# Mixture-of-experts layer: a wide expert's rows are brought out behind the next expert's gate and up product

## The chip, the cores and the metric

The kernel runs on one core of a Trainium2 chip. The metric is the time of one execution in device microseconds, taken as the median of several runs; lower is better. Five engines run programs of their own and meet through semaphores: TensorE (PE in the rows; its weight loads are PEld), VectorE (DVE), ScalarE (ACT), GpSimd (POOL) and SyncE (SP), which only issues transfers here.

## The reference

One decoder layer in float32 over 1024 tokens of width 1024. Two mixers and an output projection come first; behind them stands the part that this document is about, a feed-forward layer of 32 experts of which each token takes four:

```python
logits = xf @ router_w + router_b
top_val, top_idx = lax.top_k(logits, 4)
gates = softmax(top_val)
...
gu = xb @ w_gu[e] + b_gu[e]                  # 1024 -> 2048
gate, up = split(gu, 2)
gate = minimum(gate, 7.0); up = clip(up, -7.0, 7.0)
y = ((up + 1.0) * (gate * sigmoid(1.702 * gate))) @ w_down[e] + b_down[e]
...
out = zeros(...).at[buf_tok].add(y * buf_gate[:, None])    # sum of each token's four experts
```

The layer ends with a residual sum and a last norm.

## The kernel before

The experts are ordered by how many tokens they got, and each place in that order has a fixed number of rows (224, 204, 196, ... 98, 88). They are worked off in the order largest, smallest, second largest, second smallest, and so on (`ORDER`), so step r of the loop over 32 steps is a **wide** expert (two tiles of up to 128 rows, 132 to 224 rows together) at even r up to 28, and a **narrow** one (one tile, 88 to 128 rows) at every odd r and at r = 30. There are 15 wide ones, and each is followed by a narrow one.

TensorE's part of one step is: `gate_up` in eight blocks m = 0 to 7, each into one of four PSUM banks (`bank(m % 4)`; `gu_bank` says that a bank is free again); then `rows_in`, the transposes (line 1743) of the next expert's gathered rows; then the down product. A narrow expert's (`down_rows`, line 1778) comes out with rows on the partitions and is finished there. A wide expert's (`down`, line 1793) comes out transposed; ScalarE moves it to `yv`, and TensorE has to turn it back in `rows_out` (line 1752): for each of two tiles j, two halves of four 128x128 transposes, each half into one bank (`bank(6)` and `bank(7)`). VectorE scales a half by the gate while it moves it to `yt` (line 1919), and this gives the bank back (`tr_bank`). Both tiles use the same two banks, so the transposes of tile 1 wait for the moves of tile 0.

The rows of wide expert r are turned in step r + 1, the narrow one: TensorE does tile 0 behind block m = 3 of that step's gate and up product and tile 1 behind m = 4. VectorE's `clamps` goes through the same eight blocks one behind TensorE: two moves out of PSUM (lines 1935 and 1936; the second gives the bank back), a third operation (1939), and from m = 2 on it first waits until GpSimd has finished block m - 2 (`hT`). Its `rows_out` calls also stand behind its m = 3 and m = 4. GpSimd's `gated` makes two products for each block (1603 and 1606). Behind m = 5, `scatter_main` waits for `yt` and adds the previous expert's rows into memory (line 1594, one indirect transfer for each tile). At the head of each step GpSimd waits until the rows of the expert two steps back have landed (`y_out`), reads the list of the next expert's rows (1574) and gathers them (1581); all of that stands ahead of this step's `gated`.

The weights (12.6 MB for each expert) come in through SyncE's queue as the slots come free.

Of the kernel before, what the change touches and what calls it, by code (L numbers as in the profile page):

```python
# [30 lines left out]
ROWS = tuple(WIDTHS[r] for r in ORDER)  # L31
TILES = tuple(-(-w // P) for w in ROWS)
# [23 lines left out]
def program(nc, x, norm_mix_g, w_in, gm_norm_g, gm_ws, gm_bs, dn_conv_w, dn_a_log, dn_dt_bias,  # L56
# [6 lines left out]
    with ctx:  # L63
# [5 lines left out]
        def S(name, slot=None):  # L69
            key = name if slot is None else f"{name}_{slot}"  # L70
            if key not in sems:
                sems[key] = nc.alloc_semaphore(name=key)
            return sems[key]
# [44 lines left out]
        def cut(cols, at=None):  # L118
            a = used[0] if at is None else at
            if at is None:  # L120
                used[0] += cols
            assert a + cols <= AW, (a, cols)
            return arena[:, a:a + cols]

        def r3(ap, n):
            return ap.rearrange("p (a b) -> p a b", a=n)
# [64 lines left out]
        rec = [cut(4).rearrange("p (j c) -> p j c", j=2) for _ in range(3)]  # L191
# [4 lines left out]
        yv = r3(cut(2048), KT)  # L196
# [10 lines left out]
        def bank(n):  # L207
            return ps[:, n, :]
# [1278 lines left out]
        LAST = NE - 1  # L1487
# [10 lines left out]
        def tiles_to(r):  # L1498
            return sum(TILES[:r])

        def wide_to(r):
            return sum(n == 2 for n in TILES[:r])
# [65 lines left out]
        def _(pool):  # L1568
# [19 lines left out]
            def scatter(rows, b, n):  # L1588

                pool.wait_ge(S("yt"), b + 1)  # L1590
                pool.sem_inc(S("scattering"), 1)
                for j in range(-(-n // P)):
                    p = min(P, n - j * P)
                    pool.indirect_dma_start(h_dram, bass.IndirectOffsetOnAxis(ap=rows[0:p, j, 0:1], axis=0),  # L1594
                                            yt[0:p, j, :], None, compute_op=ALU.add).then_inc(S("y_out"), 16)
# [11 lines left out]
                    between(m)  # L1607

            def scatter_main(r, m):
                if r >= 0 and m == 5 and r + 1 < LAST:  # L1610
                    if r:
                        pool.wait_ge(S("y_out"), 16 * tiles_to(r))
                    scatter(idx[r % 3], r, ROWS[r])
# [113 lines left out]
        def _(pe):  # L1727
# [7 lines left out]
            def rows_in(b, before, wide, tiles):  # L1735

                for j in range(tiles):
                    pe.wait_ge(S("xin", j), 16 * (wide if j else b) + 16)
                    for r in range(2):
                        if j == 1:  # L1740
                            pe.wait_ge(S("gu_bank", r), 2 * b + 1)
                        for k in range(4):
                            last = t_.transpose(bank(4 * (1 - j) + r)[:, k * P:(k + 1) * P],  # L1743
                                                xin[:, j, (4 * r + k) * P:(4 * r + k + 1) * P], ident)
                        last.then_inc(S("xT_ps", r), 1)

            def rows_out(j, b, before):

                for r in range(2):
                    pe.wait_ge(S("tr_bank", r), before + (j + 1))  # L1750
                    for k in range(4):
                        last = t_.transpose(bank(6 + r)[:, k * P:(k + 1) * P], yv[:, 4 * r + k, j * P:(j + 1) * P], ident)  # L1752
                    last.then_inc(S("yt_ps", r), 1)

            def gate_up(b, n, between):

                for m in range(8):
                    g, c = m // 2, (m % 2) * P
                    pe.wait_ge(S("gu_bank", m % 4), 2 * b + m // 4 + 1)
                    for q in range(2):  # L1760
                        if m % 2 == 0:
                            pe.wait_ge(S(f"w_in{q}", g), 16 * b + 16)
                        for k in range(KT):
                            for c0, c1 in (((0, P),) if n > P else ((0, P // 2), (P // 2, P))):
                                last = t_.matmul(bank(m % 4)[c0:c1, q * CAP:q * CAP + n],  # L1765
                                                 wslot[g][:, k, 256 * q + c + c0:256 * q + c + c1],
                                                 xT[:, k, 0:n], start=(k == 0), stop=(k == KT - 1))
                    last.then_inc(S("gu_ps", m % 4), 1)
                    between(m)

            def down_rows(r):
                for q in range(2):
                    pe.wait_ge(S("w_in0", 4 + q), 16 * r + 16)
                    pe.wait_ge(S("tr_bank", q), tiles_to(r) + 1)
                    for k in range(KT):
                        if q == 0:
                            pe.wait_ge(S("hT"), 8 * r + k + 1)
                        last = t_.matmul(bank(6 + q), hT[:, k, 0:P], wslot[4 + q][:, k, :], start=(k == 0), stop=(k == KT - 1))  # L1778
                    last.then_inc(S("yt_ps", q), 1)

            def down(b, n, before, wide):
                for d in range(8):
                    g, c = 4 + d // 4, (d % 4) * P
                    if d % 4 == 0:
                        pe.wait_ge(S("w_in0", g), 16 * b + 16)
                    if d < 2:
                        pe.wait_ge(S("tr_bank", d), before + 1)
                    else:
                        pe.wait_ge(S("yv"), 8 * wide + d - 1)
                    for k in range(KT):  # L1790
                        if d == 0:
                            pe.wait_ge(S("hT"), 8 * b + k + 1)
                        last = t_.matmul(bank(6 + d % 2)[:, 0:n], wslot[g][:, k, c:c + P], hT[:, k, 0:n],  # L1793
                                         start=(k == 0), stop=(k == KT - 1))
                    last.then_inc(S("down", d % 2), 1)

            def rows_out_main(r, m):
                if r < 0 or TILES[r] == 1:
                    return
                if m == 3:  # L1800
                    pe.wait_ge(S("yv"), 8 * wide_to(r) + 8)
                    rows_out(0, r, tiles_to(r))
                if m == 4:
                    rows_out(1, r, tiles_to(r))

            rows_in(0, 0, 0, TILES[0])
            for r in range(NE):
                pe.wait_ge(S("xT_sb"), 2 * tiles_to(r + 1))
                gate_up(r, ROWS[r], lambda m: rows_out_main(r - 1, m))
                if r + 1 < NE:  # L1810
                    rows_in(r + 1, tiles_to(r + 1), wide_to(r + 1), TILES[r + 1])
                if TILES[r] == 2:
                    down(r, ROWS[r], tiles_to(r), wide_to(r))
                else:
                    down_rows(r)
# [12 lines left out]
        def _(dve):  # L1828
# [86 lines left out]
            def rows_out(j, before, of):  # L1915

                for r in range(2):
                    dve.wait_ge(S("yt_ps", r), before + (j + 1))
                    v.tensor_scalar(yt[:, j, 512 * r:512 * (r + 1)], bank(6 + r), of[:, j, 1:2], None, ALU.mult).then_inc(S("tr_bank", r), 1)  # L1919
# [25 lines left out]
            def rows_out_narrow(r):  # L1945
                dve.wait_ge(S("y_out"), 16 * tiles_to(r))
                b = narrow_to(r)
                dve.wait_ge(S("bd_in", b % 2), 16 * (b // 2 + 1))
                for q in range(2):
                    half = yt[:, 0, 512 * q:512 * (q + 1)]  # L1950
                    dve.wait_ge(S("yt_ps", q), tiles_to(r + 1))
                    v.tensor_tensor(half, bank(6 + q), bd_row[b % 2][:, 512 * q:512 * (q + 1)], ALU.add).then_inc(S("tr_bank", q), 1)
                dve.drain()
                dve.sem_inc(S("bd_used"), 1)
                v.tensor_scalar(yt[:, 0, :], yt[:, 0, :], rec[r % 3][:, 0, 1:2], None, ALU.mult).then_inc(S("yt"), 1)

            def rows_out_main(r, m):
                if r < 0:
                    return
                if TILES[r] == 1:  # L1960
                    if m == 3 and r + 1 < LAST:
                        rows_out_narrow(r)
                    return
                if m == 3:
                    if r:
                        dve.wait_ge(S("y_out"), 16 * tiles_to(r))
                    rows_out(0, tiles_to(r), rec[r % 3])
                if m == 4:
                    rows_out(1, tiles_to(r), rec[r % 3])
                    dve.drain()  # L1970
                    dve.sem_inc(S("yt"), 1)

# [134 lines left out]
```

## Time and profile before

| | |
|---|---|
| Time, median of 3 runs | 2297.16 us (2294.94 to 2298.45) |
| The profiled execution's own time | 2294.84 us |
| Its span in the profile | 2293.2 us |
| TensorE busy in the span | 97% (2216.3 us) |
| Weight loads of TensorE | 80% |
| VectorE / GpSimd / ScalarE busy | 33% / 26% / 16% |
| Granted TensorE clock, mean | 0.985 of 2.4 GHz |
| The experts' part of the span | 712 to 2293 us |

An engine's busy share tells how much of the span it had an instruction in work. The chain of waits follows the work back from the last instruction. Where TensorE is idle in the experts' part, something else sets the time there.

### The profile page before, as it was taken

The page shows a single profiled execution, that of the slowest core. Times are in us where ns is not written, and L with a number is a line of the kernel's source. Part 1 is how long each engine was busy: PE and PEld are TensorE (multiplying, and loading weights), DVE is VectorE, ACT ScalarE, POOL GpSimd, SP SyncE. Part 2 cuts the span into 40 slices and gives each one's busy share as a digit, 9 for nine tenths or more (in the row PEclk, how much of TensorE's full clock was granted, in tenths as well). Part 3 has the DMA queues.
Part 4 walks back from the last instruction along what each step waited for, and adds up shares of the span by engine and source line. Part 5 has one row for each costly group of instructions (what it writes and reads, how often), then busy time and mean ns, then how long its engine had stood idle before and what let it go on. Part 6 is the DMA issues. An engine that isn't in the chain of part 4 may idle for free.

```text
span 2293.2 us, 45352 instructions
## 1 busy us (share of the span) xinstructions
PE 2216.3 (97%) x18872; PEld 1836.1 (80%) x18873; DVE 745.9 (33%) x1759; ACT 372.1 (16%) x845; POOL 586.3 (26%) x808
## 2 busy tenths in 40 slices
PE   8999998999995999999999999999999999999997
PEld 5665447678765989898898989989889898898876
DVE  2234776445632172222212222122221222223224
ACT  2222553323320101010000101001010010010102
POOL 1133222332322122222222222222322223222222
PEclk9999999999997999999999999999999999999999
DMA  7000113011017788888979799899998979899897
GB/s 264 1 1 19 22 34 153 19 47 47 34 49 253 260 268 280 269 287 263 310 261 321 251 316 305 281 328 299 293 310 279 337 252 339 272 336 314 259 327 267
DMA packets 381978, 505.82 MB, mean 221 GB/s; under 512 B 19248, under 2 KB 295284, under 8 KB 381720
## 3 DMA queue, kind: packets, MB, share of 16 engines
q1 hardware_dynamic: 362632, 459.58, 60.0%
q0 software_dynamic: 19136, 43.29, 7.2%
q8 instruction: 151, 2.47, 0.5%
q14 instruction: 59, 0.48, 0.1%
HBM read 472.19 MB, written 33.05 MB: 220 GB/s over the span
## 4 chain that ended last, share of the span: by engine, by line
PE 58%; DMA 6%; issue 3%; POOL 1%; DVE 1%; POOLq 0%; ACT 0%; DVEq 0%; ACTq 0%; SPq 0%
PE ps L1765 35%; PE ps L1793 10%; PE ps L1778 10%; DMA h_dram<-arena 4%; PE ps L1743 2%; PE ps L1752 1%; DMA arena<-list_dram 1%; POOL arena L1606 1%; POOL arena L1603 0%; DMA arena<-h_dram 0%; DMA arena<-h_dram,arena 0%; DVE arena L1979 0%; DMA out<-arena 0%; POOL arena L1581 0%; DVE arena L1919 0%
## 5 line engine op out<-in xcount | busy, mean ns | idle before, releaser
L1765 PEld LDWEIGHTS ps<-arena 128*64 128x64 f32 (+1 forms) x12544 | 963.9, 153 | 21.3 <-issue 19.0
L1765 PE MATMUL ps<-arena 128*64 128x108 f32 (+29 forms) x12544 | 976.5, 274 | 3.2 <-issue 2.4
L1935 DVE TENSOR_SCALAR arena<-ps,arena 128x108 f32<-128x108 f32 (+29 forms) x256 | 92.3, 361 | 1080.1 <-PE ps L1765 1041.1
L1603 POOL TENSOR_TENSOR arena<-arena 128x108 f32<-128x108 f32 (+29 forms) x256 | 132.5, 517 | 719.9 <-DVEq L1942 719.8
L1675 ACT ACTIVATE arena<-arena 128x108 f32<-128x108 f32 (+29 forms) x256 | 81.5, 318 | 1194.0 <-DVE arena L1935 1191.1
L1793 PE MATMUL ps<-arena 128*128 128x224 f32 (+14 forms) x1920 | 273.4, 303 | 0.2 <-POOL arena L1606 0.2
L1793 PEld LDWEIGHTS ps<-arena 128*128 128x128 f32 x1920 | 270.4, 189 | 1.0 <-POOL arena L1606 0.4
L1778 PE MATMUL ps<-arena 128*128 128x512 f32 x544 | 236.4, 593 | 0.0
L1778 PEld LDWEIGHTS ps<-arena 128*128 128x128 f32 x544 | 102.2, 190 | 122.0 <-issue 120.6
L535 PE MATMUL ps<-arena 128*128 128x384 f32 (+1 forms) x512 | 171.1, 493 | 2.1 <-DVE arena L638 2.1
L535 PEld LDWEIGHTS ps<-arena 128*128 128x128 f32 x512 | 97.3, 193 | 67.8 <-DVE arena L638 2.4
L548 PE MATMUL ps<-arena 128*128 128x512 f32 x336 | 146.3, 593 | 0.8 <-DVE arena L685 0.8
L1606 POOL TENSOR_TENSOR arena<-arena 128x108 f32<-128x108 f32 (+29 forms) x256 | 123.0, 480 | 20.1
L548 PEld LDWEIGHTS ps<-arena 128*128 128x128 f32 x336 | 63.7, 190 | 80.3 <-issue 78.4
L1199 PE MATMUL ps<-arena 128*128 128x512 f32 x256 | 112.9, 595 | 0.8 <-DVE arena L1367 0.8
L231 POOL TENSOR_TENSOR small<-small,cst 128x4 f32<-128x4 f32 (+1 forms) x35 | 27.7, 795 | 330.6 <-DVE small L228 321.5
L1581 POOL DMA_INDIRECT arena<-h_dram,arena x47 | 47.2, 1004 | 183.3 <-DMA arena<-list_dram 161.0
L1199 PEld LDWEIGHTS ps<-arena 128*128 128x128 f32 x256 | 47.6, 190 | 56.0 <-issue 54.5
L1936 DVE TENSOR_SCALAR arena<-ps,arena 128x108 f32<-128x108 f32 (+29 forms) x256 | 90.0, 352 | 0.1
L1594 POOL DMA_INDIRECT h_dram<-arena x46 | 79.5, 1727 | 31.5 <-issue 16.6
L1022 PE MATMUL ps<-arena 128*128 128x128 f32 x640 | 83.2, 280 | 4.1 <-DVE arena L1307 2.9
L1695 ACT ACTIVATE arena<-ps,arena 128x224 f32<-128x224 f32 (+14 forms) x120 | 47.9, 399 | 231.5 <-PE ps L1793 231.5
(274 smaller groups left out, 1623.4 us busy)
## 6 DMA issues: line engine op xcount, KB each, us to landing
arena<-in_exp_w_gu SPq DMA_DIRECT2D x256, 1024.0 KB, 10.1
arena<-in_exp_w_down SPq DMA_DIRECT2D x64, 2048.0 KB, 10.5
arena<-in_exp_b_down SPq DMA_DIRECT2D x17, 512.0 KB, 10.3
arena<-in_x SPq DMA_DIRECT2D x16, 512.0 KB, 8.7
arena<-in_w_in SPq DMA_DIRECT2D x8, 1024.0 KB, 8.9
h_dram<-arena SPq DMA_DIRECT2D x16, 512.0 KB, 2.7
arena<-in_w_out SPq DMA_DIRECT2D x1, 4096.0 KB, 14.0
arena<-h_dram SPq DMA_DIRECT2D x8, 512.0 KB, 10.3
```

The lines of the kernel that those rows point to most:

```text
L535: last = t_.matmul(bank(bk)[:, to:to + width], yT[:, k, t * P:(t + 1) * P], wuvz[:, k, c0:c0 + width], start=(k == 0), stop=(k == KT - 1))
L548: last = t_.matmul(to, left[:, k, :], right[:, k, :], start=(k == 0), stop=(k == KH - 1))
L1022: last = t_.matmul(out_bank[:, c], left[:, c], right[:, c], start=start, stop=stop)
L1199: last = t_.matmul(bank(4 * s + 1 + n), mixT[s][:, k, :], wout[:, k, 512 * n:512 * (n + 1)], start=(k == 0), stop=(k == KT - 1))
L1603: v.tensor_tensor(gmn[m % 2][:, 0:n], gmn[m % 2][:, 0:n], umn[m % 2][:, 0:n], ALU.mult).then_inc(S("gum", m % 2), 1)
L1606: v.tensor_tensor(hT[:, m, 0:n], gmn[m % 2][:, 0:n], sg[m % 2][:, 0:n], ALU.mult).then_inc(S("hT"), 1)
L1675: a.activation(sg[m % 2][:, 0:n], gmn[m % 2][:, 0:n], ACT.Sigmoid, scale=ALPHA).then_inc(S("sg", m % 2), 1)
L1765: last = t_.matmul(bank(m % 4)[c0:c1, q * CAP:q * CAP + n], wslot[g][:, k, 256 * q + c + c0:256 * q + c + c1], xT[:, k, 0:n], start=(k == ...
L1778: last = t_.matmul(bank(6 + q), hT[:, k, 0:P], wslot[4 + q][:, k, :], start=(k == 0), stop=(k == KT - 1))
L1793: last = t_.matmul(bank(6 + d % 2)[:, 0:n], wslot[g][:, k, c:c + P], hT[:, k, 0:n], start=(k == 0), stop=(k == KT - 1))
L1935: v.tensor_scalar(gmn[r][:, 0:n], bank(m % 4)[:, 0:n], of[:, m:m + 1], LIMIT, ALU.add, ALU.min).then_inc(S("gmn", r), 1)
L1936: v.tensor_scalar(umn[r][:, 0:n], bank(m % 4)[:, CAP:CAP + n], of[:, 8 + m:9 + m], LIMIT, ALU.add, ALU.min)
```

## The change

TensorE no longer turns tile 0 behind block 3 and tile 1 behind block 4; it turns both behind the narrow expert's whole `gate_up`, directly ahead of `rows_in`. VectorE's moves of both tiles go behind its block m = 7, and GpSimd's scatter of a wide expert's rows goes from behind m = 5 to behind m = 7. The scatter of a narrow expert's rows stays behind m = 5, and its move on VectorE behind m = 3. No operation is added or taken away.

```diff
@@ GpSimd
             def scatter_main(r, m):
-                if r >= 0 and m == 5 and r + 1 < LAST:
+                if r >= 0 and m == (5 if TILES[r] == 1 else 7) and r + 1 < LAST:
@@ TensorE
-            def rows_out_main(r, m):
+            def rows_out_main(r):
                 if r < 0 or TILES[r] == 1:
                     return
-                if m == 3:
-                    pe.wait_ge(S("yv"), 8 * wide_to(r) + 8)
-                    rows_out(0, r, tiles_to(r))
-                if m == 4:
-                    rows_out(1, r, tiles_to(r))
+                pe.wait_ge(S("yv"), 8 * wide_to(r) + 8)
+                for j in range(2):
+                    rows_out(j, r, tiles_to(r))
...
-                gate_up(r, ROWS[r], lambda m: rows_out_main(r - 1, m))
+                gate_up(r, ROWS[r], lambda m: None)
+                rows_out_main(r - 1)
@@ VectorE
-                if m == 3:
+                if m == 7:
                     if r:
                         dve.wait_ge(S("y_out"), 16 * tiles_to(r))
-                    rows_out(0, tiles_to(r), rec[r % 3])
-                if m == 4:
-                    rows_out(1, tiles_to(r), rec[r % 3])
+                    for j in range(2):
+                        rows_out(j, tiles_to(r), rec[r % 3])
                     dve.drain()
                     dve.sem_inc(S("yt"), 1)
```

## Rows read from the trace of the kernel before

**Rows 1.** The page, part 1: busy time, share, instructions.

```profile
PE 2216.3 (97%) x18872; PEld 1836.1 (80%) x18873; DVE 745.9 (33%) x1759; ACT 372.1 (16%) x845; POOL 586.3 (26%) x808
```

**Rows 2.** Who TensorE waited for: us in total, times, longest us.

```profile
PE ps L1752 <- DVE arena L1919: 11.0, 3, 4.8
```

**Rows 3.** Timeline of TensorE in step 27 (122 rows): start us, us, engine line.

```profile
2056.49 13.55 PE L1765 MATMUL ps<-arena 128*64 128x122 f32 x256
2069.97 1.09 PE L1752 MATMUL ps<-cst,arena 128*128 128x128 f32 x8
2070.99 3.55 PE L1765 MATMUL ps<-arena 128*64 128x122 f32 x64
...
2075.50 10.22 PE L1765 MATMUL ps<-arena 128*64 128x122 f32 x192
2085.66 1.97 PE L1743 MATMUL ps<-cst,arena 128*128 128x128 f32 x16
2087.46 13.90 PE L1778 MATMUL ps<-arena 128*128 128x512 f32 x32
```

**Rows 4.** The same timeline in steps 23, 25 and 29.

```profile
1866.58 13.13 PE L1765 MATMUL ps<-arena 128*64 128x118 f32 x256
...
1897.43 1.97 PE L1743 MATMUL ps<-cst,arena 128*128 128x128 f32 x16
...
1959.85 13.34 PE L1765 MATMUL ps<-arena 128*64 128x120 f32 x256
...
1981.58 1.97 PE L1752 MATMUL ps<-cst,arena 128*128 128x128 f32 x8 [3.94 <-DVE arena L1919]
...
1995.32 1.97 PE L1743 MATMUL ps<-cst,arena 128*128 128x128 f32 x16
...
2145.55 13.77 PE L1765 MATMUL ps<-arena 128*64 128x124 f32 x256
...
2181.38 1.10 PE L1743 MATMUL ps<-cst,arena 128*128 128x128 f32 x8
```

**Rows 5.** Windows, TensorE: stretch, us, PE busy (count), granted clock, DMA share, GB/s.

```profile
1886.35:1887.60 1.25, 1.25 (x9) 1.00 0.99 377
...
1985.00:1987.00 2.00, 2.00 (x24) 0.50 1.03 323
```

**Rows 6.** Timeline of blocks 3 and 7 in step 9 (106 rows).

```profile
1217.11 0.33 DVE L1935 TENSOR_SCALAR arena<-ps,arena 128x106 f32<-128x106 f32 x1 [2.12 <-PE ps L1765]
...
1218.28 1.41 DVE L1919 TENSOR_SCALAR arena<-ps,arena 128x512 f32<-128x512 f32 x2 [0.27 <-issue]
...
1230.86 1.97 PE L1743 MATMUL ps<-cst,arena 128*128 128x128 f32 x16
1231.09 0.33 DVE L1935 TENSOR_SCALAR arena<-ps,arena 128x106 f32<-128x106 f32 x1 [2.12 <-PE ps L1765]
```

**Rows 7.** Timeline of the wait between the tiles in step 23.

```profile
1885.54 1.41 DVE L1919 TENSOR_SCALAR arena<-ps,arena 128x512 f32<-128x512 f32 x2 [0.26 <-issue]
...
1886.35 0.42 PEld L1752 LDWEIGHTS ps<-cst,arena 128*128 128x128 f32 x4 [2.46 <-DVE arena L1919]
...
1887.00 0.42 PEld L1752 LDWEIGHTS ps<-cst,arena 128*128 128x128 f32 x4 [0.24 <-DVE arena L1919]
```

**Rows 8.** The chain that ended last, ahead of step 29's wait.

```profile
2126.34 27.79 DMA h_dram<-arena
```

**Rows 9.** The scatter of step 25's 120 rows, by its line.

```profile
DMA to landing us min/median/max: 9.0/9.0/9.0
```

**Rows 10.** Timeline of VectorE in step 29, block 2.

```profile
2165.70 0.34 DVE L1936 TENSOR_SCALAR arena<-ps,arena 128x124 f32<-128x124 f32 x1
```

**Rows 11.** Timeline from the scatter of step 8's rows to step 10's first block.

```profile
1227.63 1.65 POOL L1594 DMA_INDIRECT h_dram<-arena  x1 [0.37 <-issue]
...
1245.78 1.04 POOL L1581 DMA_INDIRECT arena<-h_dram,arena  x1 [5.38 <-DMA arena<-list_dram]
...
1251.16 0.39 DVE L1935 TENSOR_SCALAR arena<-ps,arena 128x168 f32<-128x168 f32 x1 [16.33 <-PE ps L1765]
```

## The prediction

> **What bounds the kernel now.** I read the page first. TensorE is busy for 97% of the span [rows 1], so a step of the experts costs what TensorE needs for it, plus whatever TensorE waits for. Next came the list of whom TensorE waited for. In the experts' part one line of it touches the moved work: three waits of the row transposes for VectorE's moves, 11.0 us together [rows 2]. Then I laid TensorE's timeline of an undisturbed narrow step beside the three steps with those waits. The reader is to see in the first that every group starts where the last one ends [rows 3], and in the others how much longer the same stretch, from the first block to `rows_in`, takes [rows 4].
>
> **What the three waits cost.** Step 27, undisturbed, takes 2085.66 - 2056.49 = 29.17 us for that stretch [rows 3]. Step 23 takes 30.85, step 25 35.47, step 29 35.83 [rows 4]. For the undisturbed length of the other three I take the time of their first four blocks, which come ahead of the wait. Start to start these are 13.48 us in step 27 [rows 3] (0.07 less than the row's duration, which overlaps the next group), so 13.06, 13.27 and 13.70 in the three [rows 4]. In step 27 the stretch is twice 13.48 and 2.2 us for the two insertions; so the others should take 28.3, 28.7 and 29.6 us. The losses are 2.5, 6.8 and 6.2, together **15.5 us**. That is more than the 11.0 us of waiting, because behind step 25's wait of 3.94 us the clock was granted at 0.50, that is 1.2 GHz instead of 2.4, and was still there 3.4 us later; behind step 23's wait (2.46 us seen from the weight loads [rows 7]) it stayed at 1.00 [rows 5]. Step 29's wait of 4.8 us [rows 2] has its loss from both as well.
>
> Why they wait: the scatter of the narrow expert two steps back needed 27.79 us to land ahead of step 29 [rows 8] where step 25's needed 9.0 [rows 9]. GpSimd stands at the head of the step until it lands, so its block 0 comes late, VectorE's block 2 waits for it, and the move of tile 0 stands behind VectorE's block 3. TensorE, behind its own block 4, needs that move.
>
> The Trainium skill (DMA: Bandwidth & Descriptors, section Why a DMA increments its semaphore by 16 and not by 1) says that a transfer is spread over the largest number of engines, at most 16, that divides its outer size. By that rule the scatters ahead of the three waits, of 118, 118 and 122 rows, run on two engines and stay slow whatever their moment, and one of 120 rows runs on 15; by that rule, the trace agrees: 27.79 us against 9.0. Without the rule I would give the slow landings a somewhat larger chance of falling elsewhere after the change; the sum is the same.
>
> **What the change takes away.** After it TensorE has nothing of tile 0 or 1 to wait for inside `gate_up`. What can stop it there is only a bank: block 6 needs bank 2 back, which VectorE gives with line 1936 of its block 2. In step 29, the worst one, that operation ran at 2165.70 to 2166.04 [rows 10]. TensorE would reach block 6 after six blocks of 13.70/4 = 3.43 us from 2145.55 [rows 4], at 2166.1. It arrives as the bank comes free, so I count the whole 15.5 us as gone, and at most some tenths left in step 29. In steps 23 and 25 the chain is earlier against TensorE, as their shorter waits show. VectorE and GpSimd then catch up at 1.25 us for a block against TensorE's 3.4, and are in step again by block 6. If the chain ran 1 us later, the loss would be 1 us in step 29 only.
>
> **What it adds.** Today the two tiles have a whole block (3.4 us) between them, in which VectorE moves tile 0. Now nothing lies between them. I call T the moment at which TensorE leaves block 7.
> - Tile 0's eight transposes take 0.9 us from T.
> - VectorE begins its block 7 at T + 0.23 (1231.09 against 1230.86 [rows 6]). Its tile move starts 1.17 us behind the start of a block (1217.11 to 1218.28 [rows 6]): T + 1.40. The first half of tile 0 can't be moved sooner.
> - TensorE restarts 0.81 us behind the start of the move, and the second half 0.65 us later [rows 7]; four transposes take 0.45 us. So `rows_in` starts at T + 1.40 + 0.81 + 0.65 + 0.45 = T + 3.31.
> - `rows_in`'s own 16 transposes take 1.80 us as before (2085.66 to 2087.46 [rows 3]).
>
> Together 5.1 us from T to the down product. Before, the same 32 transposes cost 1.80 us plus what the two insertions cost: 1.02 us for eight (2069.97 to 2070.99 [rows 3]), twice, and about 0.1 us more, because the block between them took 2075.50 - 2070.99 - 1.02 = 3.49 us where the later ones took 3.39; together 3.95 us. The loss is 1.15 to 1.25 us, say **1.2 us in each of 15 narrow steps: 18 us**. None of it is hidden: TensorE is the bound, and `hT` and the down weights are there when `down_rows` comes. `down_rows` needs the banks of tile 1 back; VectorE moves its last half from T + 3.6 to T + 4.4, under `rows_in`, so no second wait. `rows_in`'s move into `xT` starts some 3 us later and is needed only behind the 13.7 us of `down_rows`.
>
> Bounds for that unknown wait, which no row shows in this place: if VectorE were free at once, the second tile would start one move (0.8 us) behind the first half of tile 0, and the loss is 0.6 us a step, 9 us in all. If the second tile went at the pace of steps 25 and 29, where its eight transposes took 1.9 us instead of 1.1, it is 2.0 us, 30 us in all. The rows nearest to it are step 23's at full clock, so I take 1.2.
>
> **The scatter that moves.** It waits for `yt`, now at about T + 4.6, and is issued at T + 4.8 instead of T - 3.2 (1227.63 [rows 11] against 1230.86): 8 us later, and since the next step also begins 3.3 us later seen from T, 4.7 us later seen from that step. Behind it GpSimd stands in a row: the wait for its landing, the list, the gather, then `gated` of the wide step. In step 10 GpSimd is through with the gather at 1246.8 and gets block 0 about 1.2 us behind 1251.16 [rows 11], 5.6 us of slack: 4.7 fits. A landing twice as long as that of [rows 9] would make it some 8 us late, and TensorE would not notice: it has the four banks and two blocks more, over 20 us at a wide expert's pace. Cost: nothing. Without that cover each microsecond would count in 14 steps. The rows gathered land with some 25 us to spare.
>
> **The sum.** -15.5 + 18 = +2.5 us. Against the profiled execution's 2294.84 us that is 2297.3. This execution lies 2.3 us under the median of the runs shown, so the median to expect is 2297.16 + 2.5 = 2299.7 us. A change below 0.2% (4.6 us) can't be told from none here.
>
> **The rivals.**
> 1. *The clock falls at the new place (much slower).* Between block 7 and the down product there are now 5.1 us with no product, only 32 transposes and a wait of 1.3 us. For it: after 3.94 us of waiting and eight transposes the clock was at 0.50 for 3.4 us more [rows 4, 5]. Against it: step 23's wait, followed by transposes, left it at 1.00 [rows 5, 7], and my wait is shorter. Price: step 25 lost 6.8 us with 3.94 of waiting, so 2.8 beside it; step 29 6.2 with 4.8, so 1.4. Times 15: 21 to 42 us, and with the 2.5 of the sum 2321 to 2342 us. The Trainium skill (TensorE: Matmul & The Clock Gate, Part 4: PE-mode transpose) says that transposes don't count as work for the clock; by that rule this rival would come true in most steps. Step 23 speaks against it. Chance 0.08.
> 2. *The late chain still catches TensorE (slower).* The banks come back later than I read, for instance because GpSimd also comes later through the moved scatter. If half of the 15.5 us stays: +10 us, 2307 us. It decides where block 2 on VectorE comes more than 1 us later than in [rows 10]. Chance 0.12.
> 3. *The hand-over is cheap (faster).* If VectorE takes tile 0 between its operations of block 7, or the restart is quicker, the loss nears its lower bound of 9 us: -6.5 us, 2290.7 us. It would need less than 0.73 us a step to be faster than 0.2%. Against it: VectorE works in order, and its move stands behind the whole of block 7. Chance 0.07.
> 4. *Nothing is taken away and nothing added* can't be: three waits of known place go or stay, and the tiles share two banks.
>
> **How the numbers follow.** My own case has the remaining 0.73. In it the loss per step may lie between 1.0 and 1.5 us, so +0 to +7 us: 2297 to 2304 us, of which about a quarter lies above +4.6. A quarter of 0.73 is 0.17 or 0.18. Slower: 0.08 + 0.12 + 0.17 = 0.37, of which 0.01 goes back for the near end of rival 2: 0.36. Faster: 0.07 and 0.01 of my own case: 0.08. Same: the rest, 0.56. The range 2293 to 2307 us leaves out rival 1, the far part of 2 and the near bound of 3.
>
> **What would show it.** In the profile after: no wait of line 1752 above 2 us, and steps 23, 25, 29 in line with 27; in all 15 narrow steps a wait of 1.2 to 1.5 us between the tiles, so some 20 us against VectorE's line 1919 in the list of waits; granted clock 1.00 from 725 us to the end of the last product; the wide scatter's landing ahead of the next step's first block. It would be wrong with a granted clock of 0.50 behind block 7, with waits for a bank at block 6, or with a wait between the tiles far from 1.3 us.

## The result

The changed kernel takes 2308.25 us (median of 5 runs, 2306.23 to 2311.73) against 2297.16 us: a ratio of 1.0045, 95% interval 1.0034 to 1.0057, so 11 us slower. A second set of runs gave 2308.23 against 2297.07 us, ratio 1.0054 (1.0040 to 1.0067). The prediction had 2299.7 us and a range of 2293 to 2307.

The page, and whom TensorE waited for (us in total, times, longest us), of the changed kernel:

```profile
span 2310.1 us, 45352 instructions
...
PE 2216.1 (96%) x18872; PEld 1833.6 (79%) x18873; DVE 746.7 (32%) x1759; ACT 372.3 (16%) x845; POOL 587.2 (25%) x808
```

```profile
PE ps L1752 <- DVE arena L1918: 17.0, 15, 1.5
...
PE ps L1765 <- issue: 7.2, 9, 1.5
...
PE ps L1778 <- POOL arena L1606: 2.9, 2, 2.0
...
PE ps L1765 <- DVEq L1936: 0.7, 1, 0.7
```

(VectorE's lines 1919 and 1935 are 1918 and 1934 here; 1936 is here the drain behind the second move, with which a bank is given back.) TensorE's work is the same as in [rows 1]. The three long waits of [rows 2] are gone, and in their place stand 15 short ones, one in each narrow step, of 1.1 us in the mean. The other lines are what the prediction did not have: TensorE waits inside the gate and up product with nothing that the profile can name as the releaser ("issue"; 2.4 us and five times before, 7.8 us and eight times in the second profile of the changed kernel), and in the last down product it waits for GpSimd, which it didn't before.

Laid side by side by steps, two profiled executions of the changed kernel differ from that of the kernel before in these places and nowhere else (in microseconds, worked out from the starts of TensorE's groups; the second is that of the first experiment below):

| place | predicted | first profile | second profile |
|---|---|---|---|
| beginning of the experts (first product of step 0) | 0 | +2.5 | +0.3 |
| 15 wide steps, step 30 and all down products up to step 31 | 0 | +0.1 | +0.2 |
| 12 narrow steps that were on time | +14.4 | +18.5 | +18.9 |
| steps 23, 25 and 29 | -11.9 | -11.1 | -12.2 |
| from the first product of step 31 to the end of the span | 0 | +6.9 | +5.2 |
| span | +2.5 | +16.9 | +12.4 |

The first line is not of the change: nothing before the experts was touched, and other executions began them between 716.6 and 721.7 us. The profiled execution of the changed kernel was the slowest of its five (2311.73 us). Between the two profiles of the changed kernel the steps repeat to 0.1 us where no gap of the kind "issue" stands, step 25 excepted (1.1 us shorter in the second).

Step 9 of the changed kernel shows the hand-over between the tiles:

```profile
1239.35 1.09 PE L1752 MATMUL ps<-cst,arena 128*128 128x128 f32 x8
1239.57 0.33 DVE L1934 TENSOR_SCALAR arena<-ps,arena 128x106 f32<-128x106 f32 x1 [2.41 <-PE ps L1765]
...
1240.73 2.91 DVE L1918 TENSOR_SCALAR arena<-ps,arena 128x512 f32<-128x512 f32 x4 [0.26 <-issue]
...
1241.54 1.32 PE L1752 MATMUL ps<-cst,arena 128*128 128x128 f32 x8 [1.10 <-DVE arena L1918]
...
1242.69 1.91 PE L1743 MATMUL ps<-cst,arena 128*128 128x128 f32 x16
...
1244.44 1.88 PE L1778 MATMUL ps<-arena 128*128 128x512 f32 x4
1244.51 1.64 POOL L1594 DMA_INDIRECT h_dram<-arena  x1 [2.97 <-issue]
```

With T at 1239.35: VectorE's block 7 begins at T + 0.22, the move at T + 1.38, tile 1 at T + 2.19, `rows_in` at T + 3.34, the down product at T + 5.09, and the scatter is issued at T + 5.16. The prediction had 0.23, 1.40, 2.21, 3.31, 5.1 and 4.8.

The windows over the same stretch (stretch, us, PE busy (count), granted clock, DMA share, GB/s) show the clock at 1.00, so 2.4 GHz, through 32 transposes and the wait, and in the down product behind them:

```profile
1239.35:1241.54 2.19, 1.09 (x10) 1.00 1.09 349
1241.54:1242.69 1.15, 1.15 (x8) 1.00 1.12 352
1242.69:1244.44 1.75, 1.75 (x19) 1.00 1.06 342
1244.44:1247.00 2.56, 2.56 (x8) 1.00 1.10 350
```

Steps 23 and 29 of the changed kernel run in one piece. They are to be read against [rows 4]: 1886.68 to 1916.32 is 29.6 us from the first block to `rows_in` with 3.4 us of row transposes and wait in it, where it was 30.85, and 2160.81 to 2191.46 is 30.7 us where it was 35.83.

```profile
1886.68 26.33 PE L1765 MATMUL ps<-arena 128*64 128x118 f32 x512
...
1916.32 1.91 PE L1743 MATMUL ps<-cst,arena 128*128 128x128 f32 x16
...
1999.55 6.78 PE L1765 MATMUL ps<-arena 128*64 128x120 f32 x128 [0.71 <-DVEq L1936]
...
2160.81 27.31 PE L1765 MATMUL ps<-arena 128*64 128x124 f32 x512
...
2191.46 1.04 PE L1743 MATMUL ps<-cst,arena 128*128 128x128 f32 x8
```

The one wait for a bank at block 6 came in step 25 and not, as the prediction had it, in step 29: 0.71 us in this execution, none in the second. The slow scatters kept their lengths (26.9, 28.7 and 27.6 us ahead of steps 23, 25 and 29).

### The profile page after: what moved, and what is told of

Same layout as the page of the kernel before. It is cut to its first block, busy times and chain, and to the rows that moved or that the text cites. A ratio compares the mean times of both kernels' runs of the same rounds, so it can differ in the third digit from the quotient of the medians.

```text
span 2310.1 us, 45352 instructions
## 1 busy us (share of the span) xinstructions
PE 2216.1 (96%) x18872; PEld 1833.6 (79%) x18873; DVE 746.7 (32%) x1759; ACT 372.3 (16%) x845; POOL 587.2 (25%) x808
## 4 chain that ended last, share of the span: by engine, by line
PE 55%; SPq 5%; DMA 4%; issue 3%; POOL 1%; DVE 1%; DVEq 0%; ACT 0%; POOLq 0%; ACTq 0%
PE ps L1765 35%; PE ps L1793 11%; PE ps L1778 7%; SPq L1518 3%; DMA h_dram<-arena 2%; PE ps L1743 2%; SPq L1526 1%; DMA arena<-list_dram 1%; DMA arena<-h_dram,arena 1%; PE ps L1752 1%; SPq L1536 1%; DMA arena<-h_dram 1%; DVE arena L1918 0%; POOL arena L1606 0%; POOL arena L1603 0%
## 5 line engine op out<-in xcount | busy, mean ns | idle before, releaser
L1765 PEld LDWEIGHTS ps<-arena 128*64 128x64 f32 (+1 forms) x12544 | 962.0, 152 | 23.5 <-issue 20.0
L1603 POOL TENSOR_TENSOR arena<-arena 128x108 f32<-128x108 f32 (+29 forms) x256 | 124.7, 487 | 672.6 <-DVEq L1941 672.4
L1606 POOL TENSOR_TENSOR arena<-arena 128x108 f32<-128x108 f32 (+29 forms) x256 | 123.3, 482 | 20.1
L1199 PEld LDWEIGHTS ps<-arena 128*128 128x128 f32 x256 | 47.5, 190 | 56.0 <-issue 54.5
```

Source lines behind the costliest of these rows:

```text
L1199: last = t_.matmul(bank(4 * s + 1 + n), mixT[s][:, k, :], wout[:, k, 512 * n:512 * (n + 1)], start=(k == 0), stop=(k == KT - 1))
L1603: v.tensor_tensor(gmn[m % 2][:, 0:n], gmn[m % 2][:, 0:n], umn[m % 2][:, 0:n], ALU.mult).then_inc(S("gum", m % 2), 1)
L1606: v.tensor_tensor(hT[:, m, 0:n], gmn[m % 2][:, 0:n], sg[m % 2][:, 0:n], ALU.mult).then_inc(S("hT"), 1)
L1765: last = t_.matmul(bank(m % 4)[c0:c1, q * CAP:q * CAP + n], wslot[g][:, k, 256 * q + c + c0:256 * q + c + c1], xT[:, k, 0:n], start=(k == ...
```

## The experiments

**The changed kernel again.**

> The changed kernel once more, for a second profile. Theory: the steps repeat to 0.1 us where no gap of the kind 'issue' stands (narrow steps 15 to 21 and 27 about 1.0 us longer than before, step 25 4.6 and step 29 5.2 us shorter), and the stretch from the first product of step 31 to the end is again some 5 to 7 us longer than before. The 2.5 us by which the experts began later in the first profile are not of the change and need not come again. Rival: the long end was an accident of that one execution; then the end is as before within 1 us and the time comes out near 1.003 of before.

2308.23 us, ratio 1.0054 (1.0040 to 1.0067). The steps are as in the table. The end was 5.2 us longer than before, so the long end is of the change; the late beginning of the experts (2.5 us) did not come again.

**Only the scatter moved.**

```diff
-                if r >= 0 and m == 5 and r + 1 < LAST:
+                if r >= 0 and m == (5 if TILES[r] == 1 else 7) and r + 1 < LAST:
```

> Only the scatter of a wide expert's rows goes behind m = 7; transposes and moves stay behind m = 3 and 4. Theory: the scatter's place costs nothing, since the wide step has the slack; time within 2 us of before (ratio 0.999 to 1.001), the three waits in steps 23, 25, 29 stay. Rival, that the later scatter disturbs the transfers of weights and so makes the end longer: 3 to 7 us slower, with the loss behind step 29.

2298.77 us, ratio 1.0009 (1.0000 to 1.0018). All narrow steps are within 0.7 us of before, step 31 begins at 2239.05 (2239.01 before), and the end is 54.5 us long (54.2). No stretch of the step by step account is longer by more than 0.7 us, and the three waits stand as before (11.3 us). The medians are 1.7 us apart and the interval reaches to 4 us, so the scatter's new place costs little or nothing and can't explain the 11 us.

**Step 29 left as it was.** The change in the other 14 narrow steps, with a condition `r < 28` on the places in all three programs.

```diff
+        AT_END = lambda r: r < 28
...
-                if m == 7:
+                if m == (7 if AT_END(r) else 3):
...
-                    for j in range(2):
-                        rows_out(j, tiles_to(r), rec[r % 3])
+                    rows_out(0, tiles_to(r), rec[r % 3])
+                if m == (7 if AT_END(r) else 4):
+                    rows_out(1, tiles_to(r), rec[r % 3])
```

> The change in all narrow steps but 29, which keeps transposes, moves and scatter in their old places. Theory that the transfers set the end: the 5.2 us that the change gains in step 29 are given back behind it, so leaving the gain out costs nothing: the same time as the changed kernel within 1.5 us, step 29 5 us longer and the end about 5 us shorter. Rival, that the long end has another cause (the moved scatter in general, or chance): 5 us slower than the changed kernel.

2307.84 us, ratio 1.0049 (1.0035 to 1.0063): the changed kernel's time. Step 29 took 37.6 us to its down product instead of 31.5, and the stretch from step 31 to the end 54.2 us instead of 59 to 61. So what the change gains in step 29 is worth nothing, because the end gives it back.

**Less to load for the last expert.** In the kernel before and in the changed one, seven eighths of the last expert's down weights are not loaded; the rows of that product then use the expert's weights before it.

```diff
-                    sp.dma_start(wslot[g], dn_v[ds(e, 1), :, :, 512 * (g - 4):512 * (g - 3)]...
+                    kk = 1 if isinstance(b, int) and b == LAST else KT
+                    sp.dma_start(wslot[g][:, 0:kk, :], dn_v[ds(e, 1), :, 0:kk, 512 * (g - 4):512 * (g - 3)]...
```

> The kernel before, with seven eighths of the last expert's down weights (3.5 MB of the 4 MB) not loaded, so that step 31's down product works on the expert's before it in those rows. It is the base for the next run. Theory that transfers set the end only where step 29 is quick: here step 29 is slow, the end has slack in its transfers, so little is gained: 0 to 3 us faster than before. Rival, that the transfers set the end in both kernels alike: 6 to 9 us faster (3.5 MB at some 370 GB/s are 9.5 us).

> The changed kernel with the same 3.5 MB left out. Theory: the end of the changed kernel is 5 to 7 us longer because the transfers behind step 29 run at their own pace; with 3.5 MB less the stretch from step 31's first product to the end falls from 59 to 61 us to 54 or below, and the distance to the run before it in this call falls from about 11 to about 6 us, which is what the narrow steps lose up to step 30. Rival, that the long end comes from the order of the work on VectorE and GpSimd: the distance stays at 11 us.

Before with a light end: 2297.47 us, ratio 0.9998 (0.9989 to 1.0007), nothing gained. Changed with a light end: 2302.57 us, ratio 1.0019 (1.0010 to 1.0028), so 5.1 us above its base instead of 11 (the 11 is from another set of runs, in which the kernel before took 2297.07 us; in this one it took 2298.35). The last stretch is 53.9 us long in both. TensorE's timeline of the changed kernel shows what went; first with all weights, then with the light end (its lines are one further down):

```profile
2249.02 27.74 PE L1765 MATMUL ps<-arena 128*64 128x126 f32 x512
2276.69 5.42 PE L1778 MATMUL ps<-arena 128*128 128x512 f32 x12
2283.00 1.12 PE L1778 MATMUL ps<-arena 128*128 128x512 f32 x2 [0.90 <-POOL arena L1606]
2286.11 9.69 PE L1778 MATMUL ps<-arena 128*128 128x512 f32 x18 [1.98 <-POOL arena L1606]
```

```profile
2246.85 27.74 PE L1766 MATMUL ps<-arena 128*64 128x126 f32 x512
2274.52 14.00 PE L1779 MATMUL ps<-arena 128*128 128x512 f32 x32
```

In SyncE's queue (issue times of its transfers) the reason can be followed. Of the kernel before, then of the changed one:

```profile
2160.16 29.31 SPq L1518 DMA_DIRECT2D arena<-in_exp_w_gu  x8
...
2203.60 27.00 SPq L1518 DMA_DIRECT2D arena<-in_exp_w_gu  x8
...
2240.43 7.32 SPq L1536 DMA_DIRECT2D arena<-in_exp_b_down  x1
2251.50 4.85 SPq L1540 DMA_DIRECT2D arena<-h_dram  x8
```

```profile
2175.18 29.28 SPq L1518 DMA_DIRECT2D arena<-in_exp_w_gu  x8
...
2214.96 34.61 SPq L1518 DMA_DIRECT2D arena<-in_exp_w_gu  x8
...
2257.61 5.48 SPq L1536 DMA_DIRECT2D arena<-in_exp_b_down  x1
2263.19 5.88 SPq L1540 DMA_DIRECT2D arena<-h_dram  x8
```

Both start step 30's weights 14.4 to 14.6 us into step 29 (which begins at 2145.55 and 2160.81) and need 29.3 us to issue them. From there until the queue has taken its last transfer ahead of the rows for the last sums (line 1540) it is 87.6 us before (to 2247.75) and 87.9 us after (to 2263.09), and 86.9 to 87.8 in the other kernels with all weights. The kernel before is no later for the 4.7 us that its queue stands idle ahead of step 31's weights, and the changed one no earlier for its step 29, which is 5 us quicker. The kernel that loses 5 us more in step 29 gives the queue that time. In the changed one step 31's weights take 34.61 us to issue instead of 27.00, the rows for the last sums (line 1540) start 14.2 us into step 31 instead of 12.5, and they land behind more weights: 12.25 us against 8.49 in the chain of waits. ScalarE, VectorE and GpSimd do the last norm's first part between the blocks of step 31, so GpSimd's block comes late, and TensorE waits. The chain of waits shows what the rows of line 1540 stood behind. In the kernel before it was the landing of step 30's scatter; the queue had been free for 3.7 us by then:

```profile
2241.49 10.00 DMA h_dram<-arena
...
2251.89 8.49 DMA arena<-h_dram
```

In the changed kernel it was the queue's own transfers:

```profile
2257.61 5.48 SPq L1536
...
2263.71 12.25 DMA arena<-h_dram
...
2275.98 1.06 ACT arena L1680
```

Seen from the first product of step 29, the span ends 147.7 us later in the kernel before, 149.3 and 147.6 us later in the two profiles of the changed one, and 148.5 us later in the kernel with step 29 left out, whether that step takes 31.5, 36.8 or 37.6 us to its down product. With the light end it is 147.3 us in the kernel before and 142.5 in the changed one.

**A block between the tiles, late in the step.** Tile 0 behind block 6, tile 1 behind block 7, on both engines, scatter behind m = 7.

```diff
-                if m == 3:
+                if m == 6:
                     pe.wait_ge(S("yv"), 8 * wide_to(r) + 8)
                     rows_out(0, r, tiles_to(r))
-                if m == 4:
+                if m == 7:
                     rows_out(1, r, tiles_to(r))
```

> Tile 0 is turned behind block 6 and tile 1 behind block 7, moves likewise, scatter behind m = 7. Theory: the block between the tiles hides the move of tile 0, so the wait of 1.1 us in each narrow step goes, while the three late steps keep their gain (2.5, 6 and 6 us, of which step 29's is given back at the end): about 9 us faster than the changed kernel's narrow steps imply, that is 5 to 9 us faster than before (2288 to 2293 us), less what gaps of the kind 'issue' in steps 1 to 13 take. Rival, that the hand-over is not what costs: as slow as the changed kernel.

2288.02 us, ratio 0.9959 (0.9945 to 0.9972): 9 us faster than before and 20 us faster than the changed kernel. No wait for VectorE's moves is left. Steps 5, 15, 19, 21 and 27 are 0.3 us shorter than before; steps 9, 13 and 17, also without an "issue" gap, are as before, and why is open. Steps 1, 3 and 7, where the gaps grew, are 1.5, 0.8 and 0.6 us longer. Steps 23, 25 and 29 are 2.7, 6.8 and 6.0 us shorter. The end is 61.3 us long, so here too step 29 is given back.

**The change in the three late steps alone.** As in the kernel with step 29 left out, with the condition `r in (22, 24, 28)`.

> The change only in steps 23, 25 and 29, all other narrow steps as before. Theory: step 23 1.3 us and step 25 5 to 6 us shorter, step 29 5 us shorter and given back at the end, all others unchanged to 0.1 us: 6 to 8 us faster than before (about 2290 us). Rival, that the waits removed are paid elsewhere (later gathers, later weights): within 2 us of before.

2289.36 us, ratio 0.9965 (0.9954 to 0.9977), 8 us faster by the ratio. Step 23 is 1.4 us shorter, step 25 5.2 and step 29 5.3; every other narrow step is within 0.2 us of before; the end is 60.5 us long, 6.3 more than before. The stretches of its one profile add up to a gain of 5.4 us only, so some 3 us of the gain in the medians are not explained by them.

**Fewer instructions in steps 1 and 3.** The product with 88 and 98 rows is issued 128 columns wide instead of in two halves of 64.

```diff
-                            for c0, c1 in (((0, P),) if n > P else ((0, P // 2), (P // 2, P))):
+                            for c0, c1 in (((0, P),) if n > P or n in (88, 98) else ((0, P // 2), (P // 2, P))):
```

> The changed kernel with the products of steps 1 and 3 (88 and 98 rows) issued 128 columns wide, so half as many instructions for the same work; they take longer for it, some 29 us for the product of each step instead of 21 to 23. Theory that the gaps of the kind 'issue' in steps 1 and 3 (3.3 and 1.9 us, each behind exactly 128 recorded products, which with their weight loads are 256 instructions) are TensorE waiting for its next instructions: no gap in steps 1 and 3, the gaps of step 7 stay. Rival, that they are waits for something that comes by the clock or for late weights: gaps of the same total, in the same time of the step or spaced 6.5 us apart.

Its one execution took 2316.35 us. Step 1 and a part of step 7 in the changed kernel's timeline, then the same steps in this one:

```profile
802.47 5.07 PE L1765 MATMUL ps<-arena 128*64 128x88 f32 x127 [0.29 <-issue]
809.01 5.07 PE L1765 MATMUL ps<-arena 128*64 128x88 f32 x128 [1.48 <-issue]
815.57 3.17 PE L1765 MATMUL ps<-arena 128*64 128x88 f32 x77 [1.48 <-issue]
...
1135.75 2.89 PE L1765 MATMUL ps<-arena 128*64 128x104 f32 x58 [0.69 <-issue]
```

```profile
792.14 28.71 PE L1765 MATMUL ps<-arena 128*128 128x88 f32 x256
...
1136.25 5.94 PE L1765 MATMUL ps<-arena 128*64 128x104 f32 x128 [0.50 <-issue]
1142.85 2.89 PE L1765 MATMUL ps<-arena 128*64 128x104 f32 x58 [0.67 <-issue]
```

The gaps in steps 1 and 3 are gone, those of step 7 are there. They stand 128 recorded products apart (256 instructions with the weight loads), in the middle of a block, where the program waits for nothing: a late weight or bank would show at a block's first product. Together this speaks for TensorE waiting for its next instructions in the narrowest steps, where it works through them fastest (128 products in 5.07 us at 88 rows). The queue that the profile calls "instruction" fits this: in the changed kernel's step 1 it carried one packet of 16 KB near 806.5, 813.0 and 819.5 us, as far apart as the gaps. That the instructions come from memory too late is argued from these spacings; packets asked for as the instructions are used up would be spaced so too, and no run changed their loading itself.

**Both: tiles behind 6 and 7, in steps 23, 25 and 29 alone.**

> Tile 0 behind block 6 and tile 1 behind block 7 in steps 23, 25 and 29 alone, scatter behind m = 7 there; all other narrow steps as before. Theory: step 23 2.7 us, step 25 6.8 us and step 29 6.0 us shorter than before, the last given back at the end, and steps 1 and 3 without the longer gaps that the same places brought there (1.5 and 0.8 us): 8.5 to 10 us faster than before. Rival: the 0.3 us that each other narrow step gained with tiles behind 6 and 7 counts for more, and this one is 1 to 3 us slower than the kernel with tiles behind 6 and 7 everywhere.

2287.18 us, ratio 0.9952 (0.9940 to 0.9964), the fastest kernel here, 10 us below before. Steps 23, 25 and 29 are 2.5, 6.9 and 6.1 us shorter, steps 1 and 3 within 0.3 us of before. From the kernel with these places everywhere it can't be told apart (2288.02 us in other runs).

**Tiles behind 5 and 6.**

> Tile 0 behind block 5, tile 1 behind block 6 in all narrow steps, scatter behind m = 7. Theory: a block lies between the tiles, so no hand-over wait in the steps that are on time; in step 29 VectorE is done with tile 0 about 0.5 us after TensorE asks, in step 25 not later than asked; so within 2 us of the kernel with tiles behind 6 and 7. Rival, that one block earlier already meets the late chain: waits of 2 us and more in steps 25 and 29 and 3 to 4 us slower than the kernel with tiles behind 6 and 7.

2291.46 us, ratio 0.9972 (0.9962 to 0.9983). One wait of 0.4 us for VectorE's move is left; steps 25 and 29 are 6.2 and 5.6 us shorter, steps 1 and 3 lose 1.1 and 0.5. Its median lies 3.4 us above that of the kernel with tiles behind 6 and 7, where at most 2 us were expected; the rival's number came out and its mechanism, long waits in steps 25 and 29, did not. The narrow steps together are 3.2 us longer than there: steps 23, 25 and 29 lack 1.4 us of it, and of the steps on time 5, 15, 19, 21 and 27 are as in the kernel before and don't gain the 0.3 us.

## Why the prediction was wrong

- **The hand-over between the tiles** was right in its mechanism, place and size. Predicted were waits of 1.2 to 1.5 us in 15 steps and a loss of 1.2 us a step. Measured were 15 waits of 1.0 to 1.5 us, 1.1 in the mean and so a little below what was forecast, and losses of 0.95 to 1.30 us in the steps without an "issue" gap (5, 9, 15, 17, 19, 21, 27). With both together in one place, tile 1 waits for the move of tile 0; a block between them (tiles 6 and 7) takes the wait away, and in five steps 0.3 us more.
- **The three late steps** were right too: -15.5 for the waits and +3.6 for the hand-over make -11.9; the runs show -11.1 and -12.2. With a block between the tiles, so without the hand-over, the three steps became 15.5 us shorter in the profile, as counted. One detail was off: the one wait for a bank came in step 25, not in step 29. The late scatters stayed where they were.
- **The step that failed is the sum's first term: "I count the whole 15.5 us as gone".** It was counted at TensorE, where it did go, but the 6.2 us of step 29 are not TensorE's to give; this is 5 us of the miss of 8.5. Behind that step the transfers keep their own pace (87.6 and 87.9 us for the same transfers), and the last norm waits for them; the end grew by 5.2 to 6.9 us. Three experiments show it: leaving step 29 out changed nothing (2307.84 us), a lighter load took the long end away in the changed kernel (53.9 us) and nothing in the one before, and every kernel in which step 29 is quick and all weights are loaded has an end of 59 to 61 us. The prediction's first sentence, that a step costs what TensorE needs, was taken from 97% over the span. It held up to the gate and up product of step 31, and not for the stretch behind it, which no row of the prediction looked at. Had I priced step 29 at nothing, hand-over and all, the sum would have been 14 x 1.2 - 9.3 = +7.5 us, 2304.7.
- **A term was missing**, and it is the other half of the miss. The row transposes stood in the middle of the densest stream of instructions, where eight of them take 1.0 us. Without them the narrow steps 1 to 13 wait longer for what the profile calls "issue": 7.2 us instead of 2.4, so +4.8 (+5.4 in the second profile). With it the account closes: 16.8 + 4.8 - 9.3 = 12.3 us, against 12.4 in the second profile's span and 11 in the medians. That it closes to 0.1 us is luck, since the hand-overs cost a little less than 1.2 us and the gaps of that profile a little more. That the gaps follow the place of the transposes is shown by the kernels with tiles behind 6 and 7; that they are late instructions is argued.
- **The scatter** cost nothing that could be told from none, as predicted: it was issued at T + 5.2, and moved alone it made 1.0009 (1.0000 to 1.0018).
- **The rivals.** The clock did not fall: it was at 1.00 in and behind all 15 hand-overs of both profiles. The rule of the Trainium skill (TensorE: Matmul & The Clock Gate, Part 4: PE-mode transpose) that transposes don't count as work for the clock does not show here. Rival 2, half of the 15.5 us staying, came near in size (2307 us) and was wrong in its mechanism: it looked for the loss at TensorE's banks in step 29, where nothing was lost, and not behind that step. Rival 3 fell with the hand-over.

## What to carry to other kernels

When a wait on the busiest engine goes away, ask of the last ones what other stream that wait had given time to: here a queue of weights near its limit, which sets the end. Price each removed wait up to the end of the program and not to the end of its step. And when two users of one buffer are put next to each other, the move that stood under the work between them comes into the open; keep one block between them, wherever in the step they go.

## What the runs showed that was not expected

- The float32 product of 88 rows, split into two halves of 64 columns, took 23.5 us with its gaps and 28.7 issued 128 wide. But its instructions come densely: in steps 1 and 3 TensorE stands for up to 1.5 us (1.8 in the second profile) behind every 128 recorded products, and for 0.8 us at most in the kernel before, where eight transposes stand in between. In both profiles of the changed kernel all such gaps stand in steps 1 to 13, of 88 to 108 rows; the kernel with step 29 left out has one of 0.4 us in step 17 as well.
- The clock stayed at 2.4 GHz over a stretch of 5.0 to 5.5 us with 32 transposes, no product and 1.0 to 1.5 us of waiting, in 14 places; in step 29, where the next expert is narrow too, it was 24 transposes in 4.3 us.
- The scatter of narrow rows took 24 to 29 us for 106, 118, 118 and 122 rows, 15 and 18 for 116 and 124, and 9.0 for 120, in the same places before and after the change. The Trainium skill (DMA: Bandwidth & Descriptors, section Why a DMA increments its semaphore by 16 and not by 1) lets the number of engines follow the divisors of the rows, and these landings agree. Those of 118, 118 and 122 rows are what makes steps 23, 25 and 29 late in the first place; that of 106 rows landed 1 us ahead of step 11 and held nothing up.
